# Weight loads and read-backs that are issued only when the one two ahead has landed

## What is computed

```python
def moe(h, router_w, router_b, w1, w3, w2):
    ...
    experts = gidx * EXPERTS_PER_GROUP + local       # 2 of 32 experts for each of 1024 tokens
    weights = top_p / jnp.sum(top_p, axis=-1, keepdims=True)
    ...
    def expert_block(args):
        xb, e = args
        return (jax.nn.silu(xb @ w1[e]) * (xb @ w3[e])) @ w2[e]
    ...
    out = jnp.einsum('nk,nkd->nd', weights.astype(h.dtype), y_assign)

def reference(...):
    ...
        x = x + gt2 * moe(h, router_w, router_b, exp_w1[l], exp_w3[l], exp_w2[l])
    return rmsnorm(x, g_final)
```

## Time and profile before

| | us |
|---|---|
| median of 3 runs | 1118.53 (1116.23 to 1118.76) |
| the profiled execution | 1118.2 |
| its span | 1116.4 |
| PE busy in the span | 1003.4 (90%) |
| DVE, ACT, POOL busy | 567.8, 344.5, 147.2 |
| mean DMA rate over the span | 265 GB/s |
| share of weight loads in the chain that ended last | 10% |

### The profile page before, as it was taken

How to read it: one execution, slowest core, us unless ns; L and a number is a source line. 1 busy time by engine, 2 the same in 40 slices (tenths; PEclk the granted TensorE clock), 3 DMA queues, 4 the chain that set the end, 5 groups by cost and what they waited for, 6 DMA issues and landing times.

```text
span 1116.4 us, 12725 instructions
## 1 busy us (share of the span) xinstructions
PE 1003.4 (90%) x4904; PEld 666.3 (60%) x4904; DVE 567.8 (51%) x881; ACT 344.5 (31%) x489; POOL 147.2 (13%) x133
## 2 busy tenths in 40 slices
PE   4798999999999999985899999999999989999820
PEld 2477988878898455554666564646555554654500
DVE  2588643424652244554674463635454462544547
ACT  5511125222222121121652433425142252423212
POOL 2000000001100001103112122112022011100112
PEclk9899999999999999995899999999999999999965
DMA  9829411111304464424589999999999999999655
GB/s 371 298 75 359 169 39 38 38 38 40 114 1 173 167 243 172 170 95 160 188 323 352 411 425 425 428 427 426 426 427 425 424 418 409 422 392 375 255 237 224
DMA packets 52560, 295.82 MB, mean 265 GB/s; under 512 B 11130, under 2 KB 23435, under 8 KB 36115
## 3 DMA queue, kind: packets, MB, share of 16 engines
q1 hardware_dynamic: 43634, 274.00, 61.5%
q0 software_dynamic: 7712, 16.80, 4.0%
q10 hardware_dynamic: 1152, 4.19, 0.9%
HBM read 278.55 MB, written 25.85 MB: 273 GB/s over the span
## 4 chain that ended last, share of the span: by engine, by line
PE 72%; DMA 14%; DVE 7%; ACT 3%; issue 2%; DVEq 1%; POOL 1%; SPq 0%; ACTq 0%; POOLq 0%
PE bank L954 10%; DMA place_dt_float<-in_exp_w_dram 10%; PE bank L1096 9%; PE bank L1077 6%; PE bank L1072 5%; PE bank L1066 4%; PE bank L1069 4%; PE bank L795 4%; PE bank L790 4%; PE bank L792 3%; PE bank L791 3%; PE bank L796 3%; PE bank L797 3%; DVE place_dt_float32r L1860 3%; PE bank L1102 2%
## 5 line engine op out<-in xcount | busy, mean ns | idle before, releaser
L1860 DVE TENSOR_TENSOR place_dt_float32r<-place_dt_float,place_dt_float32r 128x4096 fp32r<-128x4096 f32 x36 | 159.1, 4419 | 46.0 <-ACT place_dt_float32r L1345 46.0
L1345 ACT CAST place_dt_float32r<-place_dt_float 128x4096 fp32r<-128x4096 f32 x36 | 130.2, 3615 | 153.0 <-DMA place_dt_float<-in_exp_w_dram 116.7
L1096 PE MATMUL bank<-place_dt_float,arena 128*128 128x512 f32 x288 | 127.9, 597 | 1.7 <-issue 1.7
L691 POOL DMA_INDIRECT y_dram<-arena,slot_i x25 | 65.1, 2603 | 429.0 <-DVE arena L1871 429.0
L954 PE MATMUL bank<-arena 128*128 128x512 f32 x256 | 114.6, 602 | 0.1
L1077 PE MATMUL bank<-place_dt_float,tail_dt_float 128*64 128x512 f32 x448 | 99.2, 595 | 0.0
L607 POOL TENSOR_TENSOR stats<-stats,half 128x1 f32<-128x1 f32 (+1 forms) x34 | 31.1, 916 | 482.0 <-DVE stats L1391 455.2
L795 PE MATMUL bank<-low_r 128*128 128x256 f32 (+1 forms) x320 | 93.7, 293 | 0.0
L1096 PEld LDWEIGHTS bank<-place_dt_float,arena 128*128 128x128 f32 x288 | 53.3, 190 | 63.8 <-issue 62.2
L796 PE MATMUL bank<-low_r 128*128 128x256 f32 (+1 forms) x320 | 90.8, 284 | 0.0
L797 PE MATMUL bank<-low_r 128*128 128x256 f32 (+1 forms) x320 | 90.8, 284 | 0.0
(11 more groups left out here) (253 smaller groups left out, 1410.2 us busy)
## 6 DMA issues: line engine op xcount, KB each, us to landing
place_dt_float<-in_exp_w_dram SPq DMA_DIRECT2D x96, 2048.0 KB, 23.6
arena<-in_w_ada_dram SPq DMA_DIRECT2D x24, 1024.0 KB, 9.1
low<-in_w_in_dram SPq DMA_DIRECT2D x11, 1024.0 KB, 5.5
arena<-y_dram SPq DMA_DIRECT2D x3, 2048.0 KB, 16.9
arena<-in_x_dram SPq DMA_DIRECT2D x2, 2048.0 KB, 12.1
arena<-in_w_out_dram SPq DMA_DIRECT2D x2, 2048.0 KB, 7.9
arena<-in_x_dram SPq DMA_DIRECT2D x8, 512.0 KB, 3.7
x_dram<-arena SPq DMA_DIRECT2D x8, 512.0 KB, 2.6
```

The source lines that it names most:

```text
L1096: mm = pe.matmul(bank[5 + j][:], hT_sb[:, k, :], ws[0][:, k, cols], start=(k == 0), stop=(k == KF - 1))
L1345: act.copy(part_hi[0 if kind == "w1" else 1], alias[F32][n % SLOTS]).then_inc(S["w_hi"], 1)
L1860: TT(alias[F32R][n], alias[F32][n], part_hi[j].bitcast(F32), ALU.subtract).then_inc(S["w_lo"], 1)
```

## The change

Two waits are added on SyncE's queue. In `load_unit`, a load from number 8 on waits, besides for its slot, until load n-2 has landed. In the last stage the read-back of piece h waits from the third piece on until piece h-2 has landed.

```diff
@@ -521,6 +521,9 @@
                 if n >= SLOTS:
                     before_kind, before_pass, _ = stream[n - SLOTS]
                     sp.wait_ge(S[{"w1": "h1_mm", "w2": "y_mm", "w3": "h3_mm"}[before_kind]], before_pass + 1)
+
+                    b = n - 2
+                    sp.wait_ge(w_ld[b % SLOTS], w_ld_was[b % SLOTS] + 16 * (b // SLOTS) + 16)
                 v = {"w1": w1_v, "w2": w2_v, "w3": w3_v}[kind]
                 sp.dma_start(slot[s], one(v, e)).then_inc(w_ld[s], 16)
 
@@ -585,6 +588,8 @@
             for h in range(2):
                 sp.wait_ge(scat[h], 16 * ((PASSES + 1 - h) // 2))
             for h, (a, b) in enumerate(y_parts):
+                if h >= 2:
+                    sp.wait_ge(y_ld[h - 2], y_ld_was[h - 2] + 16)
                 sp.dma_start(yy[:, a:b, :], y_t[:, a:b, :]).then_inc(y_ld[h], 16)
             sp.wait_ge(out_st, 16 * TILES)
```

## The result

| | before | changed |
|---|---|---|
| median, us | 1118.53 (1116.23 to 1119.28, 5 runs) | 1121.42 (1120.66 to 1123.71, 5 runs) |
| ratio, 95% interval | | 1.0031 (1.0016 to 1.0045) |
| again, on another occasion | 1118.70 (19 runs) | 1123.31 (8 runs), ratio 1.0042 (1.0027 to 1.0057) |
| profiled execution, us | 1118.2 | 1120.66 |
| its span | 1116.4 | 1118.9 |

The changed kernel is slower by 3 to 5 us, 0.31 and 0.42%. That is inside the range, and right at the 0.3% up to which I called a change "the same". In the profiled executions it is 2.5 us. In the changed kernel the lines behind the first edit are numbered 3 higher and those behind the second 5 higher.

A forecast was written before the change was run, and what follows sets the result against it. Weight landings, set by the DMA engine that finishes last, were taken to bound the later expert stage. Terms 0 + 0 + 0.9 us on the profiled 1118.2, with runs' median 0.3 higher, gave 1119.4 us, range 1115.5 to 1124.

The forecast's parts named there:

- the term I had put at 0: Expert stage: the wait on the load two before costs 0, with ends of -3 and +4 us.
- What bounds the kernel: Expert stage, 802 to 1041 us: weight landings set the end; bringing them forward gains at most 9.6 us.
- The sum of 251.8 us: Loads 48 to 94: 46 loads at 4.9 us plus 22 gathers and scatters at 1.2, against 254.8 measured.
- A packet isn't cheaper when the others are idle: Argument against rival 2: 403 GB/s per full share from 1047 to 1060 us, 420 in the full stretch.
- Rival 2: Expert stage, faster: engines share one limit, so a shorter queue speeds the last one; 1110 us, chance 0.08.
- The change in the expert stage: Up to 76 weight loads are issued later, still in time for the last engine; cost 0.
- The new lead of 4.5 us is longer: Weight loads: issue 4.5 us ahead of the previous landing suffices, since load 19 lost nothing at 3.8.
- the round trip: Weight loads: lone load plus issue takes 8.5 us at most; two on their way allow one per 4.25, below 4.9.
- The rule against the change: Skill's advice to issue DMAs early; its fit gave 6.8 us per lone load, so two on their way suffice.
- Rival 1: Expert stage, slower: with two loads on their way the window runs dry; +11 us, 1131, chance 0.14.
- The loads behind the last weights: Residual and g_final after load 95: issued near 1037, 8 us later, with 16 us of cover; cost 0.
- The read-back: Last stage: third piece waits for the first, issued near 1076.8; +0.9 us, ends 0 and +1.4.

The follow-up runs named there:

- e1_loads: Only the weight loads' wait on the load two before, against the kernel before; read-back unchanged: 1122.71 us, ratio 1.0038.
- e7_rows: Kernel before with gather token numbers clamped, so rows past an expert's count are read too: 1118.69 us, ratio 1.0002.
- e4_one: Kernel before with each weight load waiting for the load one before to land, one on its way: 1344.05 us, ratio 1.2013.
- f3_no_rows_late: Kernel before without gathered or scattered rows from pass 2 and one split product, plus wait on n-2 and two delaying reads: 1117.24 us.
- e2_readback: Only the wait in the read-back, against the kernel before; weight loads unchanged: 1119.08 us, ratio 1.0010.

## Why the prediction was right or wrong

**The sign and the size.** Forecast 1119.4, range 1115.5 to 1124.0; measured 1121.42, and 1123.31 the second time. The range held it. The likeliest case, no measurable change, was a little off: it is slower by 0.31 to 0.42%, with both intervals clear of zero. That the range held is in part luck: e1_loads alone is just past the end of the term I had put at 0, and what kept it there is named below.

**What bounds the kernel.** Right. The DMA engine that ends last sets the landings, it has next to no pause, and less queue in front of it gives nothing back. e7_rows bears it out: 4.7 MB more at no cost that can be told. The sum of 251.8 us took every gather and scatter as full, which can hold for that engine alone. "A packet isn't cheaper when the others are idle" held as well (the median is 0.61 us in e4_one too), but another thing was overlooked: with less queue more packets are slow. Rival 2 fell with e7_rows, where 425 GB/s were moved and nothing was gained.

**The change in the expert stage.** This step failed, in its size. I took 0 with ends of -3 and +4; e1_loads has +4.2, just past the upper end. The failed sentence is "The new lead of 4.5 us is longer": the lead of 3.8 us that was "with no loss" came from one load, 19, and one load doesn't make a threshold. At leads of some 4.2 us a load loses 0.5 in the mean (f3_no_rows_late), at 4.8 about 0.06, and single loads with 3.9 and 4.1 us lost nothing there either. The second argument, the round trip, failed too: it took a lone load's 7.7 to 8.1 us, as if the start and the end of a load were hidden behind the one beside it. With 4.2 us of the other to come and 4.9 of its own bytes a load would take 9.1 us, and it takes 9.6. The window of two was not at 8.5 of 9.8 us but right at the edge. What saved the change was a number that I had taken too high on the safe side: the issue follows a landing by 0.12 us, not 0.4, which left a lead of 4.8 us or more instead of 4.5. By f3_no_rows_late 0.6 us less lead than that cost 35 us.

The rule against the change, to issue a DMA early, was right in its direction: every later issue was slower, by 1.5, 4.2, 23, 67 and 226 us. The estimate beside it was not: a lone 2 MB load takes 8.0 us in e4_one instead of 6.8, and two on their way weren't enough to earn the same as five. The fit behind the 6.8 us stands in the Trainium skill (DMA: Bandwidth & Descriptors, Anatomy of one DMA — SWDGE (gpsimd) path) for DMAs that GpSimd issues, and these come from SyncE.

**Rival 1, the window runs dry.** Its mechanism is the one that acts, at somewhat over a third of its price (+4.2 against +11 us), and its chance of 0.14 was too low for a margin that I had from one row. It named the decisive quantity, the round trip against two intervals, with the wrong value in it.

**The loads behind the last weights.** Right: issued at 1038.45 (said: near 1037), hidden; SyncE is held for 3.28 us, not 10.

**The read-back.** Right in kind. Said: a wait of 1.3 us before the third tile, +0.9. Measured: 0.94 us in the changed kernel, 1.08 in e2_readback, so +0.6 and +0.7, and 1119.08 against 1118.50 by the medians of that occasion. The third piece took 8.0 us, as said; what was too large is again the 0.4 us for the issue: by the trace it was issued 0.01 us after the first had landed.

**The signs to look for.** The median from issue to landing is 10.6 (said 11). TensorE has 228.49 us in the second stretch (said 229). Load 48 lands at 787.6 against 786.9 before; load 94 has no record of its landing, and load 95 lands 1.5 us later. The third piece is issued at 1078.3, not 1076.8, since the whole read-back starts 1.9 us later. One thing I thought possible did not come: gathers land no sooner with the shorter queue, 15.8 us in the median here, from 787 to 1041 us, where it was 15.7:

```profile
L688 POOL DMA_INDIRECT arena<-xn_dram,slot_tok x10: 1017/1019/1021, 793.1 to 990.3; - x10
...
DMA to landing us min/median/max: 15.5/15.8/16.8
```

**What stays open.** Why a packet takes longer at a start (1.21 instead of 0.61 us in e4_one), and whether each slow one later on follows an empty engine: the records don't name the engine. In the changed kernel a packet is longer by 0.023 us in the mean. With 128 packets to a load, 8 for each engine, 71 loads would make that 13 us, and the pace grew by 2.1 to 5.6 in the executions with this wait and the rows as before; so more than half of it would fall on engines that aren't the last. A wait on only a part of the 16 increments would have measured the lead more finely; it wasn't tried.

## What to carry to other kernels

A queue of loads needs to be only so deep that the DMA engine that ends last never runs empty, and extra bytes on engines that wait for it cost nothing that could be told here (4.7 MB in e7_rows). But where the queue's depth is tied to landings, find the lead at which loads begin to cost from many loads in a row, or by delaying the issue on purpose, never from a single one and never from a lone load: here 4.8 us cost 0.06 us per load in the mean, 4.2 us cost 0.5. Of two and three on their way, three (+1.5 us) is the safer choice, and neither beats leaving the slots alone to set the pace.

## What the runs showed of the hardware

- Without rows in the traffic a 2 MB load costs 4.94 us with some five on their way, and 5.00 us with two, each issued when the one two before lands; 1.1 us of delay in the issue brings 5.44 us. One at a time, with rows, it is 8.29 us.
- A packet of 16 KB takes 0.61 us in a full queue; the first 16 packets of a load that starts on empty engines take 1.21 us in the median (e4_one).
- A DMA doesn't end on all engines at once: with several loads queued, packets of the DMAs behind load 95 started up to 17 us before it had landed.
- The DMA share is no measure of throughput: a share of 0.99 went with 386, 391 and 412 GB/s, 1.01 with 412, 424 and 425.
- After a landing SyncE's next DMA was issued 0.12 us later.
- A gather of up to 128 rows beside the weights takes 15.8 us with two weight loads in the other queue and 15.7 us with five.
- With one load on its way TensorE's granted clock fell as well, to 0.86 in the stretch from 802 us (0.99 before): the same stretch has 620 matmuls in 174.86 us, 0.28 us each, against 951 in 229.37 us before, 0.24 us each. So its idle time has a second price.

```profile
802.00:1041.00 239.00, 174.86 (x620) 94.71 (x620) 75.30 (x75) 51.65 (x49) 20.94 (x14) 0.86 0.73 274
```
